# A one-layer hybrid decoder trunk: the S5 read-out in two calls of four column groups instead of four calls of two, and three pieces of work in another order

## The chip, the cores and the metric

The kernel runs on one core of a Trainium2 chip. The metric is the device time of one execution in microseconds (us). Before the change the median of three runs is 482.74 us (482.57 to 483.27). One further execution was profiled; every row below is from it, and it took 482.97 us.

A core has five engines with instruction streams of their own: PE (TensorE, matrix products), DVE (VectorE), ACT (ScalarE), POOL (GpSimd) and SP (SyncE, which only issues DMAs here). They wait for each other through semaphores, which are written out by hand in this kernel. Within an engine the order of the program is the order of execution.

## The reference, cut to what matters

The layer takes x (256 tokens by 1024) and 256 memory tokens. One input projection feeds four groups of 256 channels each: S5 (a diagonal complex state-space model), mLSTM, RWKV-7 and MoBA attention. Each group is normed, they are joined and projected out; then come a cross-attention into the memory and a SwiGLU feed-forward.

The part that the change rewrites is the last step of S5. The complex states are read out through `c`:

```
y = (jnp.einsum('blgp,ghp->blgh', xs_re, c_re) - jnp.einsum('blgp,ghp->blgh', xs_im, c_im))
y = y.reshape(bsz, seq, GW) + d_skip * u
z = jax.nn.gelu(y)
return z * jax.nn.sigmoid(z @ w_glu + b_glu)
```

RWKV-7 is computed in two chunks of 128 tokens with a triangular inverse that is built level by level (levels 1 to 5, then a corner). MoBA has one block of 256 keys here, so it is causal attention with a relative bias.

## The kernel before, in words

**Weights.** Each weight is split into a high part (ACT, `high_part`, L379) and a rest (DVE, `rest`, L385, one instruction of 128x1024), and a product is three passes: high by high, high by rest, rest by high. The splits go through few buffers, so that ACT waits for PE to have used one, DVE for ACT, and PE for DVE. `rests(n)` on DVE and `highs(n)` on ACT do the splits up to the n-th half weight.

**S5 before the read-out.** 1024 complex states are eight tiles of 128. They are handled in four pairs, q = 0 to 3. For each pair PE makes the driving terms (`s5_in`), ACT copies them out, POOL (DVE for q = 2) turns them by the angle of the time (`rotate`), DVE scans them over time (`scan(q)`, L1879 and L1880, four instructions), and POOL turns them back (`rotate_back(q)`, L1166, four products of 128x512 into `pr`). `rotate_back(1)` also waits for `h_rest` 4, which DVE signals behind the second four of its `mem_rest` instructions (L1945, the rest of the normed memory).

**The read-out.** `s5_out(q, b)` on PE takes the two state tiles of pair q and makes their 32 output channels each, in bank 3: four terms for each tile, eight matmuls of 128 rows by 32 columns of weights with 256 moving columns. Each writes 32 of the 128 output partitions (a column group of the array); two groups are in use in one call. A float32 matmul is two records in the profile, so a call is 16 records. It waits for `rotated_back` q + 1. `rotate_back(q)` overwrites `pr` and waits for `s5_out_used` q in its turn, so read-outs and turns alternate.

**RWKV levels.** `level_p(n, c, b)` on PE waits for `rw_level_mask`, which POOL's `level_mask(n)` (L1176, two instructions) signals; `level_x(n, c)` follows and DVE's `level_update(n)` (L1906, L1908) subtracts. On POOL the order is: `rotate_back(0)`, mask 3, `rotate(1)`, mask 4, `rotate_back(1)`, mask 5, `rotate_back(2)`, `rotate(3)`, `rotate_back(3)`.

**PE's order around the change** (L780 to L900): level 2's `level_x`; `s5_out(0)`; level 3's `level_p`; the transposes `g_col` (L804) and the rows `max_row` for mLSTM; the projection `mb_v`; level 3's `level_x`; `wkv(0)` in two halves (the keys of the memory) with level 4 between; `s5_out(1)`; `ml_qk(2)`, `ml_qk(3)`; level 5's `level_p`; `wkv(1)`; ... `mb_scores(0)` to `(2)`; `s5_out(2)`; `mb_scores(3)`; `solve_u(0)`; first half of `wkv(3)`; `S0`; `bonus`; `s5_out(3)`; second half of `wkv(3)`; ... `values_low(0)`; `solve_u(1)`; `values_low(1)`.

**DVE's order around the change** (L2056 to L2100): the RWKV right side (L2022), the last scan `scan(3)`, `corner()` (L1915, two instructions), `mem_keys(2)` (L1954, the copy of the third quarter of the keys), `mb_biased(0)` to `(2)` (L2033, L2034), a weight rest (L385), `mb_biased(3)`, `solution(0)` (L2026, the first RWKV solution's copy out of its bank, which PE's `S0` waits for), and two reductions (L2064, L2065) that give `mb_max`. ACT's eight exponentials wait for `mb_max`; behind them on ACT stands the weight high of `values_low(0)`. DVE goes on with the S5 output's GELU (L2078 to L2088), and the weight rest that `values_low(1)` needs stands behind those.

Of the kernel before, what the change touches and what calls it, by code (L numbers as in the profile page):

```python
# [14 lines left out]
T = 256  # L15
# [71 lines left out]
def trunk_kernel(nc, x_t, x_rows, mem_t, consts_d, params_d, weights_d, gains_d, rel_scratch, out):  # L87
    ctx = ExitStack()
    with ctx:
# [84 lines left out]
        bu, pr = v4(bu_, 2, T), v4(pr_, 2, T)  # L174
# [130 lines left out]
        def free_of(name):  # L305
            return free[uses[name][0]]
# [105 lines left out]
        def _(pe):  # L412
# [145 lines left out]
            def s5_out(q, b):  # L558

                o = pe_open(pe, "s5_y", b) if q == 0 else bank[b]  # L560
                pe.wait_ge(S["rotated_back"], q + 1)
                for n, (w, x) in enumerate(((c_re, 0), (c_nre, 1), (c_im, 2), (c_im, 3))):
                    for i in (2 * q, 2 * q + 1):
                        y = o[32 * (i % 4):32 * (i % 4) + 32, (i // 4) * T:(i // 4 + 1) * T]
                        last = mm(y, w[:, i, :], pr[:, x, i % 2, :], n == 0, n == 3)
                last.then_inc(full[b] if q == 3 else S["s5_out_used"], 1)
# [230 lines left out]
            s5_out(0, 3)  # L797

            level_p(3, 0, 4)
            level_p(3, 1, 6)  # L800
# [16 lines left out]
            for h in range(NH):  # L817
                max_row(h)
            split_values(11, "mb_v", 0, h_split)
# [12 lines left out]
            s5_out(1, 3)  # L832
# [4 lines left out]
            level_p(5, 1, 6)  # L837
            wkv(1, 1)
# [25 lines left out]
            s5_out(2, 3)  # L864

# [15 lines left out]
            s5_out(3, 3)  # L881
# [235 lines left out]
        def _(pool):  # L1117
# [39 lines left out]
            def rotate_back(q):  # L1157

                cq, sq = cos[:, 2 * q:2 * q + 2, :], sin[:, 2 * q:2 * q + 2, :]
                pool.wait_ge(S["scanned"], q + 1)  # L1160
                if q == 1:
                    pool.wait_ge(S["h_rest"], 4)
                if q > 0:
                    pool.wait_ge(S["s5_out_used"], q)
                for x, (a_, b_) in enumerate(((cq, t1), (sq, t2), (cq, t2), (sq, t1))):
                    last = g.tensor_tensor(pr[:, x], a_, b_, ALU.mult)  # L1166
                last.then_inc(S["rotated_back"], 1)
# [33 lines left out]
        def _(act):  # L1201
# [194 lines left out]
            level_evac(3)  # L1396
            o = wait_full(act, "g_col")
            a.activation(gcol, o[:, 0:8], ACT.Copy).then_inc(free_of("g_col"), 1)
            highs(H_WKV + 1)
# [259 lines left out]
        def _(dve):  # L1659
# [393 lines left out]
            scan(3)  # L2053
            corner()
            mem_keys(2)
            mb_biased(0)  # L2056
            mb_biased(1)
            mb_biased(2)
            rests(H_WKV + 8)
            mb_biased(3)  # L2060
            solution(0)
# [372 lines left out]
```

## Time and profile before

| what | us |
|---|---|
| median of three runs | 482.74 |
| the profiled execution | 482.97 |
| its span, first to last instruction | 481.2 |
| PE busy | 471.1 (98%) |
| DVE busy | 345.4 (72%) |
| ACT busy | 270.6 (56%) |
| POOL busy | 108.4 (23%) |

The span is 1.8 us shorter than the time of the same execution. PE's matmuls are pipelined, and the end of each is modelled, so busy PE doesn't say that no wait is hidden. A row of the timeline gives start and length, engine, line, operation, out<-in, how many were merged, and in brackets the idle time of the engine just before it with what ended it. All of PE's products in the stretch are on one line (L414, a helper), so they are told apart by their tiles and shapes: 128*32 is a read-out, 64*64 an RWKV level. The chain of waits follows the work that ended last back through what released it.

### The profile page before, as it was taken

What the parts mean: (1) busy time and instruction counts of PE and PEld (TensorE: products, weight loads), DVE (VectorE), ACT (ScalarE), POOL (GpSimd) and SP (SyncE); (2) the same over time, 40 slices, a digit from 0 to 9 for tenths busy, and PEclk for the clock granted to TensorE, in tenths of its full rate; (3) what the DMA queues carried; (4) which work ended last, traced back from release to release, by engine and by line L of the source; (5) the groups of instructions that cost most, each with busy time, mean ns of one, the idle gap of its engine ahead of it and who ended that gap; (6) DMA issues with size and microseconds to landing.
All of it is one profiled execution on the core that took longest, in us unless ns stands there. A gap on an engine that the chain in (4) does not pass through costs nothing.

```text
span 481.2 us, 8231 instructions
## 1 busy us (share of the span) xinstructions
PE 471.1 (98%) x3330; PEld 409.0 (85%) x3330; DVE 345.4 (72%) x488; ACT 270.6 (56%) x442; POOL 108.4 (23%) x75
## 2 busy tenths in 40 slices
PE   8999999999999999999999999999999999999995
PEld 6999888989888877889998887888888888888884
DVE  3899999999889887888455736767676777642234
ACT  5678884417232347679557556655555555453342
POOL 0005427793576600000000000000000000344450
PEclk9999999999999999999999999999999999999999
DMA  7874429221410226263733532465555455455502
GB/s 267 338 314 168 161 89 340 69 99 50 148 71 20 89 89 262 86 246 123 260 116 133 207 143 88 176 218 185 196 209 198 176 176 185 172 194 217 193 0 87
DMA packets 12697, 78.91 MB, mean 164 GB/s; under 512 B 1487, under 2 KB 2164, under 8 KB 4084
## 3 DMA queue, kind: packets, MB, share of 16 engines
q1 hardware_dynamic: 12660, 78.39, 45.4%
q8 instruction: 26, 0.43, 0.4%
q14 instruction: 11, 0.09, 0.1%
HBM read 77.33 MB, written 1.84 MB: 165 GB/s over the span
## 4 chain that ended last, share of the span: by engine, by line
PE 70%; DVE 19%; issue 3%; ACT 3%; DMA 2%; POOL 1%; SPq 1%; DVEq 0%; ACTq 0%
PE bank L414 69%; DVE we_rest L385 3%; DMA ring<-weights 2%; POOL arena L1166 1%; DVE arena L1742 1%; DVE wm_rest L385 1%; DVE bank L1689 1%; ACT we_high L379 1%; ACT arena L1440 1%; DVE arena L2014 1%; DVE wk_rest L385 1%; DVE h L1945 0%; DVE arena L397 0%; DVE arena L1759 0%; DVE arena L1879 0%
## 5 line engine op out<-in xcount | busy, mean ns | idle before, releaser
L414 PE MATMUL bank<-h,w_high 128*128 128x512 f32 (+1 forms) x392 | 120.4, 372 | 0.0
L379 ACT ACTIVATE w_high<-ring 128x1024 fp32r<-128x1024 f32 x63 | 66.2, 1058 | 62.7 <-PE bank L414 59.2
L385 DVE TENSOR_TENSOR w_rest<-ring,w_high 128x1024 fp32r<-128x1024 f32 x51 | 63.3, 1245 | 49.2 <-ACT w_high L379 49.0
L414 PE MATMUL bank<-h,w_rest 128*128 128x256 f32 x320 | 89.6, 280 | 0.0
L414 PEld LDWEIGHTS bank<-h,w_high 128*128 128x128 f32 x392 | 68.7, 188 | 13.6 <-issue 0.4
L385 POOL TENSOR_TENSOR w_rest<-ring,w_high 128x1024 fp32r<-128x1024 f32 x7 | 16.8, 2400 | 259.5 <-ACT w_high L379 259.5
L414 PEld LDWEIGHTS bank<-h,w_rest 128*128 128x128 f32 x320 | 60.5, 189 | 0.0
L414 PE MATMUL bank<-arena 64*64 64x64 f32 (+8 forms) x794 | 51.3, 253 | 1.6 <-POOL arena L1119 1.1
L385 DVE TENSOR_TENSOR w_rest<-third_slot,w_high 128x1024 fp32r<-128x1024 f32 x27 | 32.7, 1222 | 27.3 <-ACT w_high L379 27.2
L414 PEld LDWEIGHTS bank<-arena 64*64 64x64 f32 (+4 forms) x794 | 42.2, 144 | 11.4 <-issue 3.9
L414 PE MATMUL bank<-h,we_high 128*128 128x256 f32 x256 | 47.2, 287 | 2.1 <-DVE we_rest L385 1.6
L379 ACT ACTIVATE w_high<-third_slot 128x1024 fp32r<-128x1024 f32 x30 | 31.2, 1055 | 21.0 <-PE bank L414 20.8
L414 PEld LDWEIGHTS bank<-h,we_high 128*128 128x128 f32 x256 | 40.0, 192 | 3.4 <-issue 1.6
L414 PE MATMUL bank<-h,we_rest 128*128 128x256 f32 x128 | 36.2, 283 | 0.0
L414 PE MATMUL bank<-w_high,act_rest 128*128 128x512 f32 x80 | 31.1, 389 | 0.0
L414 PE MATMUL bank<-w_rest,act_high 128*128 128x512 f32 x80 | 31.1, 389 | 0.0
L414 PE MATMUL bank<-w_high,act_high 128*128 128x512 f32 x80 | 31.1, 389 | 0.0
L1166 POOL TENSOR_TENSOR arena<-arena 128x512 f32<-128x512 f32 x16 | 25.0, 1594 | 20.6 <-DVE arena L1880 8.4
L414 PE MATMUL bank<-w_high,h 128*128 128x512 f32 x88 | 27.9, 403 | 0.6 <-DVE w_high L385 0.6
L385 DVE TENSOR_TENSOR we_rest<-ring,we_high 128x1024 fp32r<-128x1024 f32 x18 | 23.9, 1343 | 1.7 <-ACT we_high L379 1.6
L414 PEld LDWEIGHTS bank<-h,we_rest 128*128 128x128 f32 x128 | 24.5, 192 | 0.0
L414 PEld LDWEIGHTS bank<-w_high,h 128*128 128x128 f32 x88 | 16.5, 188 | 4.7 <-DVE w_high L385 0.7
(341 smaller groups left out, 1020.2 us busy)
## 6 DMA issues: line engine op xcount, KB each, us to landing
ring<-weights SPq DMA_DIRECT2D x49, 1024.0 KB, 4.8
third_slot<-weights SPq DMA_DIRECT2D x15, 1024.0 KB, 4.8
gain<-gains SPq DMA_DIRECT2D x3, 512.0 KB, 5.6
cst<-consts SPq DMA_DIRECT2D x1, 1216.0 KB, 8.8
par<-params SPq DMA_DIRECT2D x1, 1168.0 KB, 10.4
kx<-x_t SPq DMA_DIRECT2D x2, 512.0 KB, 5.6
ring<-weights SPq DMA_DIRECT2D x2, 512.0 KB, 6.6
vx<-mem_t SPq DMA_DIRECT2D x1, 1024.0 KB, 9.7
```

What stands on the lines that cost most here:

```text
L379: nc.scalar.activation(split_half(i)[0], raw_half(i), ACT.Copy).then_inc(S["w_high"], 1)
L385: e.tensor_tensor(rest_, raw_half(i), high.bitcast(F32), ALU.subtract).then_inc(rest_done(i)[0], 1)
L414: return nc.tensor.matmul(out_, lhsT, rhs, start=start, stop=stop, skip_group_check=True)
L1166: last = g.tensor_tensor(pr[:, x], a_, b_, ALU.mult)
L1440: e = a.activation(Sm[:, h, lo:hi], Sm[:, h, lo:hi], ACT.Exp, bias=nmax[:, 4 * m + h:4 * m + h + 1], accum_out=mb_sum[:, 4 * m + h:4 * m + ...
L1689: v.tensor_tensor(o, o, copies(rstd_x[0:rows_], n), ALU.mult).then_inc(S["x_scaled"], 1)
L1742: last = v.scalar_tensor_tensor(cv[:, i, d:T], o[:, c, 0:T - d], cw[:, i, 3 - d:4 - d], cv[:, i, d:T], ALU.mult, ALU.add)
L2014: v.reciprocal(den, den).then_inc(S["ml_den"], 1)
```

## The change

- **PE:** `s5_out` takes j = 0, 1 in place of q. A call waits for `rotated_back` 2j + 2, covers four state tiles, and each of its four terms goes to four column groups (output partitions 32g, g = 0 to 3). `s5_out(0)` now stands behind level 5's `level_p`, and `s5_out(1)` where `s5_out(3)` was; two of the four places are gone. Level 3's `level_p` moves behind `g_col` and `max_row`.
- **POOL:** `rotate_back` writes to two buffers in turn, `pr` and the space of `vx` (which holds the memory until its split is done). `rotate_back(1)` waits for no read-out any more; `(2)` and `(3)` wait for `s5_out_used` 1.
- **ACT:** the copy of `g_col` comes ahead of the copies of level 3's products.
- **DVE:** `scan(3)` moves behind `corner()` and `mem_keys(2)`; `solution(0)` moves ahead of a weight rest and `mb_biased(3)`.

The number of matmuls, of POOL's products and of DVE's and ACT's instructions stays the same.

```diff
-        bu, pr = v4(bu_, 2, T), v4(pr_, 2, T)
+        bu = v4(bu_, 2, T)
+        prs = [v4(pr_, 2, T), v4(flat(vx), 2, T)]
...
-            def s5_out(q, b):
-
-                o = pe_open(pe, "s5_y", b) if q == 0 else bank[b]
-                pe.wait_ge(S["rotated_back"], q + 1)
+            def s5_out(j, b):
+
+                o = bank[b] if j else pe_open(pe, "s5_y", b)
+                pe.wait_ge(S["rotated_back"], 2 * j + 2)
                 for n, (w, x) in enumerate(((c_re, 0), (c_nre, 1), (c_im, 2), (c_im, 3))):
-                    for i in (2 * q, 2 * q + 1):
-                        y = o[32 * (i % 4):32 * (i % 4) + 32, (i // 4) * T:(i // 4 + 1) * T]
-                        last = mm(y, w[:, i, :], pr[:, x, i % 2, :], n == 0, n == 3)
-                last.then_inc(full[b] if q == 3 else S["s5_out_used"], 1)
+                    for g in range(4):
+                        last = mm(o[32 * g:32 * g + 32, j * T:(j + 1) * T], w[:, 4 * j + g, :],
+                                  prs[g // 2][:, x, g % 2, :], n == 0, n == 3)
+                last.then_inc(full[b] if j else S["s5_out_used"], 1)
...
             level_x(2, 1)
-            s5_out(0, 3)
-
-            level_p(3, 0, 4)
-            level_p(3, 1, 6)
...
             for h in range(NH):
                 max_row(h)
+            level_p(3, 0, 4)
+            level_p(3, 1, 6)
             split_values(11, "mb_v", 0, h_split)
...
             level_x(4, 1)
-            s5_out(1, 3)
...
             level_p(5, 1, 6)
+            s5_out(0, 3)
             wkv(1, 1)
...
             mb_scores(2, 2)
-            s5_out(2, 3)
-
             mb_scores(3, 5)
...
-            s5_out(3, 3)
+            s5_out(1, 3)
             wkv(3, 1, (1,))
...
-                if q > 0:
-                    pool.wait_ge(S["s5_out_used"], q)
+                if q > 1:
+                    pool.wait_ge(S["s5_out_used"], 1)
                 for x, (a_, b_) in enumerate(((cq, t1), (sq, t2), (cq, t2), (sq, t1))):
-                    last = g.tensor_tensor(pr[:, x], a_, b_, ALU.mult)
+                    last = g.tensor_tensor(prs[q % 2][:, x], a_, b_, ALU.mult)
...
-            level_evac(3)
             o = wait_full(act, "g_col")
             a.activation(gcol, o[:, 0:8], ACT.Copy).then_inc(free_of("g_col"), 1)
+            level_evac(3)
...
             solve_rhs(0)
-            scan(3)
             corner()
             mem_keys(2)
+            scan(3)
             mb_biased(0)
             mb_biased(1)
             mb_biased(2)
+            solution(0)
             rests(H_WKV + 8)
             mb_biased(3)
-            solution(0)
```

PE's order at the second read-out, before. The first row is the last of level 4's `level_x`; the rows of 32x256 are `s5_out(1)`, those that wait for `ml_qk` are `ml_qk(2)` and `(3)`, and those that wait for `rw_level_mask` are the two calls of level 5's `level_p`.

```order
L414 MATMUL bank<-arena 64x64 [waits bank_free6]
L414 MATMUL bank<-arena 64x64 x7
L414 MATMUL bank<-arena,par 32x256 [waits rotated_back]
L414 MATMUL bank<-arena,par 32x256
L414 MATMUL bank<-arena 32x256 x2
L414 MATMUL bank<-arena,par 32x256 x4
L414 MATMUL bank<-arena 128x256 [waits ml_qk,bank_free2]
...
L414 MATMUL bank<-arena 64x64 [waits bank_free5,rw_level_mask,bank_free4]
L414 MATMUL bank<-arena 64x64 x7
L414 MATMUL bank<-arena 64x64 [waits bank_free7,rw_level_mask,bank_free6]
L414 MATMUL bank<-arena 64x64 x7
L414 MATMUL bank<-h,wm_high 128x256 [waits w_rest_mid,bank_free1]
```

And PE's order in the same place after the change, from level 5's second `level_p` on:

```order
L415 MATMUL bank<-arena 64x64 [waits bank_free7,rw_level_mask,bank_free6]
L415 MATMUL bank<-arena 64x64 x7
L415 MATMUL bank<-arena,par 32x256 [waits rotated_back,bank_free3]
L415 MATMUL bank<-arena,par 32x256
L415 MATMUL bank<-vx,par 32x256 x2
L415 MATMUL bank<-arena 32x256 x2
L415 MATMUL bank<-vx,arena 32x256 x2
L415 MATMUL bank<-arena,par 32x256 x2
L415 MATMUL bank<-vx,par 32x256 x2
L415 MATMUL bank<-arena,par 32x256 x2
L415 MATMUL bank<-vx,par 32x256 x2
L415 MATMUL bank<-h,wm_high 128x256 [waits w_rest_mid,bank_free1]
```

The read-out of eight matmuls ahead of `ml_qk(2)` is gone, and one of sixteen, half of them from `vx`, stands between level 5's products and `wkv(1)`.

DVE's order before, from the RWKV right side (the row that waits for `bank_full5`) to the reductions. The rows that wait for `rw_top` are `corner()`, the row into `kx` is `mem_keys(2)`, the COPY is `solution(0)`.

```order
L2022 TENSOR_SCALAR arena<-bank 128x256 [waits bank_full5]
L1879 SCALAR_TENSOR_TENSOR arena<-small,arena 128x256 [waits rotating]
...
L1915 TENSOR_SCALAR arena<-bank 64x256 [waits rw_top,bank_full4]
L1915 TENSOR_SCALAR arena<-bank 64x256 [waits rw_top,bank_full6]
L1954 TENSOR_TENSOR kx<-bank,arena 128x512 [waits rstd_m,bank_full1]
...
L385 TENSOR_TENSOR w_high<-ring,w_high 128x1024 [waits w_high]
L2033 SCALAR_TENSOR_TENSOR arena<-bank,small,arena 128x128 [waits rstd_col,rel_in,bank_full5]
L2034 SCALAR_TENSOR_TENSOR arena<-bank,small,arena 128x256
L2026 COPY arena<-bank 128x256 [waits bank_full4]
L2064 TENSOR_REDUCE small<-arena 128x4 [waits bank_free2,bank_free5,bank_free0,bank_free7]
```

And after:

```order
L2019 TENSOR_SCALAR arena<-bank 128x256 [waits bank_full5]
L1912 TENSOR_SCALAR arena<-bank 64x256 [waits rw_top,bank_full4]
L1912 TENSOR_SCALAR arena<-bank 64x256 [waits rw_top,bank_full6]
L1951 TENSOR_TENSOR kx<-bank,arena 128x512 [waits rstd_m,bank_full1]
L1876 SCALAR_TENSOR_TENSOR arena<-small,arena 128x256 [waits rotating]
...
L2023 COPY arena<-bank 128x256 [waits bank_full4]
L386 TENSOR_TENSOR w_high<-ring,w_high 128x1024 [waits w_high]
L2030 SCALAR_TENSOR_TENSOR arena<-bank,small,arena 128x128 [waits rstd_col,rel_in,bank_full5]
L2031 SCALAR_TENSOR_TENSOR arena<-bank,small,arena 128x256
L2061 TENSOR_REDUCE small<-arena 128x4 [waits bank_free2,bank_free5,bank_free0,bank_free7]
```

The scan has gone behind three instructions, and the copy ahead of the weight rest; the work between the right side and the reductions is the same.

## Rows read from the trace of the kernel before

**Rows 1.** The page, parts 1 and 2: busy times, and PE's granted clock in tenths.

```profile
PE 471.1 (98%) x3330; PEld 409.0 (85%) x3330; DVE 345.4 (72%) x488; ACT 270.6 (56%) x442; POOL 108.4 (23%) x75
...
PEclk9999999999999999999999999999999999999999
```

**Rows 2.** The chain of waits: start, us, what.

```profile
119.55 6.00 POOL arena L1166 x4
...
125.60 16.76 PE bank L414 x212
...
310.69 165.28 PE bank L414 x872
```

**Rows 3.** Timeline of PE: start, us, instruction, [idle before <-releaser].

```profile
35.58 0.47 PE L414 MATMUL bank<-h,we_high 128*128 128x256 f32 x2 [0.97 <-DVE we_rest L385]
...
101.81 1.34 PE L414 MATMUL bank<-arena 64*64 64x64 f32 x32 [0.17 <-DVE arena L1908]
...
104.94 0.47 PE L414 MATMUL bank<-wm_high,h 128*128 128x256 f32 x1
...
125.60 0.62 PE L414 MATMUL bank<-arena,par 128*32 128x256 f32 x4 [0.58 <-POOL arena L1166]
...
127.45 2.01 PE L414 MATMUL bank<-arena 64*128 64x256 f32 x40
129.39 0.50 PE L414 MATMUL bank<-h,wm_high 128*128 128x256 f32 x2
...
161.45 0.63 PE L414 MATMUL bank<-arena,par 128*32 128x256 f32 x4
...
171.78 1.28 PE L414 MATMUL bank<-arena 64*64 64x64 f32 x16
173.62 0.50 PE L414 MATMUL bank<-w_high,h 128*128 128x512 f32 x1 [0.56 <-DVE w_high L385]
```

**Rows 4.** Timeline of POOL.

```profile
101.60 5.38 POOL L1152 TENSOR_TENSOR arena<-arena 128x512 f32<-128x512 f32 x1
...
108.31 1.30 POOL L1155 TENSOR_TENSOR arena<-arena 128x512 f32<-128x512 f32 x1
...
126.10 0.64 POOL L1176 TENSOR_TENSOR arena<-arena,cst 128x256 f32<-128x256 f32 x1
...
148.91 1.29 POOL L1155 TENSOR_TENSOR arena<-arena 128x512 f32<-128x512 f32 x1
154.83 5.98 POOL L1166 TENSOR_TENSOR arena<-arena 128x512 f32<-128x512 f32 x4 [4.64 <-PE bank L414]
157.29 2.29 POOL L1166 TENSOR_TENSOR arena<-arena 128x512 f32<-128x512 f32 x1
```

**Rows 5.** Timeline of DVE.

```profile
102.34 1.21 DVE L385 TENSOR_TENSOR wm_rest<-ring,wm_high 128x1024 fp32r<-128x1024 f32 x1
...
109.34 1.34 DVE L385 TENSOR_TENSOR wm_rest<-ring,wm_high 128x1024 fp32r<-128x1024 f32 x1 [0.70 <-ACT wm_high L379]
...
117.76 1.66 DVE L1945 SCALAR_TENSOR_TENSOR h<-vx,par,h 128x256 fp32r<-128x256 f32 x4
...
149.20 2.08 DVE L385 TENSOR_TENSOR wm_rest<-ring,wm_high 128x1024 fp32r<-128x1024 f32 x1
...
153.88 0.72 DVE L1915 TENSOR_SCALAR arena<-bank 64x256 f32<-64x256 f32 x2
...
155.12 0.33 DVE L2033 SCALAR_TENSOR_TENSOR arena<-bank,small,arena 128x128 f32<-128x128 f32 x1
...
157.07 1.35 DVE L385 TENSOR_TENSOR w_high<-ring,w_high 128x1024 fp32r<-128x1024 f32 x1
...
159.00 0.41 DVE L2026 COPY arena<-bank 128x256 f32<-128x256 f32 x1
159.33 0.67 DVE L2064 TENSOR_REDUCE small<-arena 128x4 f32<-128x512 f32 x1
159.92 1.20 DVE L2065 TENSOR_REDUCE small<-arena 128x4 f32<-128x1024 f32 x1
```

## The prediction

> **What bounds the kernel now.** The page first. PE is busy for 471.1 of 481.2 us and its granted clock is full in all 40 slices [rows 1]. That invites the reading that every microsecond taken from PE is one won. The chain of waits tests it. Its last piece is 165.28 us of products from 310.69 on [rows 2]: there PE alone sets the time, and whatever shift it has on entering is carried to the end. In the stretch that the change touches (99 to 174 us), the chain goes through POOL's `rotate_back(1)` at 119.55 to PE at 125.60 [rows 2]. So third, the waits: PE's timeline shows its two real stops there, 0.58 us before the read-out at 125.60 (POOL) and 0.56 us before 173.62 (DVE's weight rest) [rows 3]. At 173.62 PE is late because DVE is. The question is therefore what the change does to the DVE and POOL work that ends there, not what it does to PE's sum.
>
> Fourth, the two timelines side by side, since DVE and POOL hold each other up. DVE's weight rest takes 1.21 us undisturbed (102.34). The one at 109.34 takes 1.34, the one at 149.20 2.08, the one at 157.07 1.35 [rows 5]. POOL's product open at each start ends at 109.61, 150.20 and, as the next one starts at 157.29, about 157.3 [rows 4]. Each rest ends 1.08 us behind that (110.68, 151.28, 158.42). In the other direction POOL's product at 157.29 takes 2.29 and ends 1.16 behind the rest. So whichever is under way finishes, and the other then needs its own time less some 0.15. A DVE rest that comes early into an open POOL product wins nothing.
>
> **The change part by part.** A read-out call takes 1.85 us of PE (125.60 to 127.45 [rows 3]). Four calls become two. If four column groups run side by side as two do, a call still takes 1.85: PE's work falls by 3.70 us. If they run as pairs, one after the other, two calls take what four did: 0. I take 1.85 and keep both ends. By stretch:
>
> 1. *99.7 to 104.9, first read-out gone, level 3 behind the rows.* `mb_v` starts at 104.94 and could start 1.85 and the wait of 0.17 earlier, at 102.92 at best. Its first half frees the buffer whose rest DVE starts at 109.34, behind 0.70 us of idling [rows 5]. DVE could start at 108.64. But POOL's product at 108.31 is open until 109.61 [rows 4], so the rest would end at 110.69, as before. Gain 0; bounds 0 and 0.70. ACT's copy of `g_col` ahead of level 3's copies only keeps `max_row` supplied, and has the same cover.
>
> 2. *To the second read-out.* DVE has no idle time from there to the end of its memory rests at 119.42 (117.76 + 1.66), where `h_rest` 4 releases `rotate_back(1)` on POOL at 119.55 [rows 2, 5]. Both are unchanged. POOL ends it at 125.55 and makes level 5's masks until 126.74 (126.10 + 0.64 [rows 4]). PE no longer waits for the turn, but its new neighbour, level 5's `level_p`, waits for the mask: even with no gain before, PE would be there at 125.02 (125.60 less the stop) plus 0.86 for the `ml_qk` pair. The second half of `level_p` starts at 126.80, takes 0.62 (under half of the 1.34 of such a pair [rows 3]), and the first new read-out 1.85: `wkv(1)` starts at 129.27, where it was 129.39 [rows 3]. Gain 0.1. The stop has changed its releaser, and what was removed ahead of it is spent waiting.
>
> 3. *129 to 151.3.* The 0.1 travels with PE to DVE's mLSTM output. There the rest at 149.20 is held by POOL's product from 148.91 to 150.20 [rows 4, 5], and that one hangs on `scan(2)` and `rotated_back` 2, which have not moved. The rest ends at 151.28 either way. Gain 0. The same 0.9 us of holding would swallow most of a loss of that size.
>
> 4. *151.3 to 161.1, DVE's new order.* `corner` and `mem_keys(2)` take 1.24 (153.88 to 155.12 [rows 5]). With the last scan behind them, `scanned` 4 comes at 155.19, not 153.95. POOL's `rotate_back(3)` used to start at 154.83, kept from starting by the third read-out on PE [rows 4]; now it starts at 155.27, 0.44 later, so removing that wait is more than given back. Its third product would start near 157.73, and its second ends at 157.78. DVE now does `solution(0)` first (0.33, 159.00 to 159.33 [rows 5]), comes to the rest at 157.39, is held to 157.78 and ends it at 158.86, before at 158.42. `mb_biased(3)` follows (0.65) and the reductions can start at 159.55 instead of 159.33; they end at 161.34 instead of 161.12 (159.92 + 1.20). Loss 0.22.
>
> 5. *The last read-out.* POOL's turn takes 5.98 [rows 4] with one rest in it: `rotated_back` 4 at 161.25. PE has by then lost one call and moved up by about 2 us, so it waits some 1.8 us in front of `s5_out(1)` and starts it at 161.3, before at 161.45 [rows 3]. The copy of the first solution ends at 157.47 and PE needs it at about 157.8: no stop. Gain 0.15 on PE, which reaches the old stop at 172.9 (before 171.78 + 1.28 = 173.06 [rows 3]).
>
> 6. *161.3 to 173.6.* ACT's exponentials, DVE's reciprocal, the S5 output and two rests follow `mb_max` without a change, and POOL's work among them hangs on the same signal. The rest comes 0.22 later, PE resumes at 173.84, and the stop grows from 0.56 to about 0.95.
>
> Sum: 0.22 later on the path: 482.97 + 0.22 = 483.2 for such a profiled execution. That one stood 0.23 above the median, so 482.9 to 483.0 for a median of runs. No DMA is moved past another; SP's order is the same.
>
> One rule of the Trainium skill bears on terms 1 and 3. In SBUF — State Buffer, "SBUF: two separate sides", a DVE instruction with two SBUF inputs and a GpSimd instruction that reads SBUF exclude each other for the whole instruction, whoever starts first. By that rule the gain of term 1 is 0. One pair of rows speaks against it: the rest at 102.34 takes 1.21 although POOL's L1152 is open from 101.60 to 106.98 [rows 4, 5], where three other pairs agree. If term 1 went by that pair, its gain would be 0.70; this is the second rival.
>
> **The rivals.**
>
> *A, nothing won (forecast).* Terms as above: 482.9, own range 482.4 to 483.5.
>
> *B, POOL doesn't hold DVE at 108.6.* The rest starts 0.70 earlier, the memory rests and POOL's turn and masks with it, and the whole rhythm moves up; less term 4's 0.22 it is 0.5: 482.2. For it: the pair at 102.34. Against: the three others, and that POOL's delayed product would then hold the memory rests behind it.
>
> *C, PE's work counts.* If the masks don't bind (POOL ahead of what its rough spans show), PE comes to `wkv(1)` earlier by the first call with its wait (2.0), the second with its stop (2.4), less one new call (1.85): 2.6. DVE's 0.2 off: 480.4. For it: PE at 98%. Against: `h_rest` 4 at 119.42, which POOL cannot pass, and DVE without a gap before it.
>
> *D, slower: the four groups run as two pairs.* Each call is 3.6. The first sends PE on 1.6 later, of which DVE's output keeps about 0.5 after the holding at 149.2; the last starts at 161.7 instead of 161.3 and ends at 165.3. PE then comes to the stop near 174.9, later than the rest, so PE decides: 1.3 later, 484.1. It decides as soon as a call costs over about 2.8 us. For it: no row shows four tiles of 128 rows at once. Against: two such tiles take the time of one now. In TensorE: Matmul & The Clock Gate, "Measured speedup vs the span model", three column tiles run 2.38 times as fast as in turn; by that the call would be some 2.3, and the sum the same.
>
> *E, slower: the clock falls in the new idle time of 1.8 us.* The longest stop now is 0.97 (35.58 [rows 3]) with the clock at full level. At the lower level (1.2 GHz for 2.4) PE's 11 us to the stop would take twice that: some 494.
>
> **How the numbers follow.** A 0.57, B 0.14, C 0.12, D 0.13, E 0.02, and 0.02 for what isn't listed. This kernel can tell about 0.2% (0.97 us) from no change: faster is below 481.8, slower above 483.7. Faster takes C and a little of B: 0.15. Slower takes D, E and the tail of A: 0.20. No change: 0.65. The range reaches down past B and halfway to C, and up over D: 481.4 to 484.3, which leaves out most of C, E and odd cases, under 0.2 in all.
>
> **What would show it.** In the changed profile: each read-out call 1.85 to 1.9 us long with four starts a few nanoseconds apart (against D); the rest of `wkv(0)`'s first half starting near 108.6 and ending at 110.7 (against B); PE's stop before level 5's `level_p`, released by POOL's L1173, with the mask ending near 126.7 (against C); `wkv(1)` at 129.3; DVE's rest at about 157.4 ending near 158.9; `mb_max` at 161.3; PE idle for 1.8 us before the last read-out, at full clock; PE's stop at 173.8 nearly 1 us long. I am wrong if `rotate_back(1)` starts before 119.4, or if `mb_max` comes before 161.

## The result, and the profile after

| | median us | lowest to highest | runs |
|---|---|---|---|
| before | 483.04 | 482.51 to 483.52 | 20 |
| changed | 483.56 | 482.94 to 484.46 | 20 |

The ratio is 1.0014, 95% interval 1.0008 to 1.0021: 0.4 to 1.0 us slower. I had forecast 0.2 slower (482.9, range 481.4 to 484.3, no measurable change the likeliest). The direction held, the range held, and the size was too small. The profiled execution of the changed kernel took 483.12, with a span of 481.3, 0.1 over that of before. Yet it ran 0.23 us ahead when it came to the changed stretch: the weight rest near 42 us, where both kernels are the same, starts at 41.75 instead of 41.98 already. So I measure from a mark that both have: the start of the weight rest near 102 us (102.34 before, 102.11 after).

The page's busy times and granted clock, which answer to [rows 1]:

```profile
PE 468.0 (97%) x3330; PEld 407.3 (85%) x3330; DVE 345.9 (72%) x488; ACT 270.5 (56%) x442; POOL 108.4 (23%) x75
...
PEclk9999999999999999999999999999999999999998
```

PE is busy for 3.1 us less. The four column groups do run side by side. PE's timeline at the two read-outs and at the two stops, which answers to [rows 3]:

```profile
126.03 1.28 PE L415 MATMUL bank<-arena 64*64 64x64 f32 x32 [0.73 <-issue]
127.24 0.41 PE L415 MATMUL bank<-arena,par 128*32 128x256 f32 x2
127.26 0.41 PE L415 MATMUL bank<-vx,par 128*32 128x256 f32 x2
127.48 0.39 PE L415 MATMUL bank<-arena,par 128*32 128x256 f32 x2
...
129.11 0.50 PE L415 MATMUL bank<-h,wm_high 128*128 128x256 f32 x2
...
157.39 0.70 PE L415 MATMUL bank<-arena 128*64 128x64 f32 x16 [0.45 <-DVE arena L2023]
158.02 1.13 PE L415 MATMUL bank<-arena,cst 128*128 128x512 f32 x2
161.12 0.41 PE L415 MATMUL bank<-arena,par 128*32 128x256 f32 x2 [1.97 <-POOL vx L1163]
...
173.82 0.73 PE L415 MATMUL bank<-w_high,h 128*128 128x512 f32 x2 [1.07 <-DVE w_high L386]
```

A call runs from 127.24 to 129.11, 1.87 us, and the pair from `arena` and the pair from `vx` start together. That rules out rival D. What PE gained comes back as idle time, which stands in brackets: 0.73 ahead of level 5's products, 0.45 ahead of `S0`, 1.97 ahead of the last read-out, 1.07 ahead of `values_low(1)` (before 0.56). Two more stops of 0.44 and 0.65 us, at 103.47 and 112.96, are new as well; both are released by DVE. The profile puts down no engine as the releaser of the 0.73 ("issue"), where I had said POOL's mask. The rows still fit the mask: its two instructions end at 125.93 and 126.53, and the two halves of level 5's products start 0.10 behind each.

The chain of waits, which answers to [rows 2] (start, us, what):

```profile
117.61 1.59 DVE h L1942 x4
...
119.34 5.97 PE bank L415 x96
125.31 0.73 issue
126.03 16.05 PE bank L415 x220
...
148.99 1.66 DVE wm_rest L386
...
157.21 1.50 DVE w_high L386
...
160.10 1.22 DVE small L2062
...
161.35 1.03 ACT arena L1437 x5
```

The chain no longer passes through POOL's turn at 119.55. From 142 to 161.3 no engine but DVE is on it. POOL's and DVE's timelines at the places of [rows 4, 5]:

```profile
148.71 1.30 POOL L1152 TENSOR_TENSOR arena<-arena 128x512 f32<-128x512 f32 x1
155.10 5.96 POOL L1163 TENSOR_TENSOR vx<-arena 128x512 f32<-128x512 f32 x4 [5.09 <-DVE arena L1877]
156.35 1.28 POOL L1163 TENSOR_TENSOR vx<-arena 128x512 f32<-128x512 f32 x1
157.59 2.25 POOL L1163 TENSOR_TENSOR vx<-arena 128x512 f32<-128x512 f32 x1
```

```profile
108.33 2.14 DVE L386 TENSOR_TENSOR wm_rest<-ring,wm_high 128x1024 fp32r<-128x1024 f32 x1
...
148.99 2.10 DVE L386 TENSOR_TENSOR wm_rest<-ring,wm_high 128x1024 fp32r<-128x1024 f32 x1
...
156.88 0.40 DVE L2023 COPY arena<-bank 128x256 f32<-128x256 f32 x1
157.21 1.50 DVE L386 TENSOR_TENSOR w_high<-ring,w_high 128x1024 fp32r<-128x1024 f32 x1
158.64 0.34 DVE L2030 SCALAR_TENSOR_TENSOR arena<-bank,small,arena 128x128 f32<-128x128 f32 x1
158.90 0.47 DVE L2031 SCALAR_TENSOR_TENSOR arena<-bank,small,arena 128x256 f32<-128x256 f32 x1
159.50 0.69 DVE L2061 TENSOR_REDUCE small<-arena 128x4 f32<-128x512 f32 x1
160.10 1.21 DVE L2062 TENSOR_REDUCE small<-arena 128x4 f32<-128x1024 f32 x1
```

The rest at 108.33 starts 6.21 behind the mark, where it was 7.00, and takes 2.14: it ends at 110.47, 8.35 behind the mark; before it was 8.34. The rest at 157.21 is held until 157.63 and ends at 158.71.

**Three marks for all runs.** Between four points the traces repeat to 0.02 us, so that single executions can be compared: the start of the rest near 102; the start of the rest near 149; the end of the second reduction; the first product of `values_low(1)`. The pieces between them are a, b and c. Behind the last of the points the traces are alike again: 307.5 to 307.6 us to the end of the span in thirteen of the fourteen. Ahead of the first they are not: it comes between 101.9 and 103.4 us, and that scatter is in every median. The last columns are the median and ratio over all runs (before, on the same chips, 482.94 to 483.07).

| kernel | a | b | c | median | ratio, 95% interval |
|---|---|---|---|---|---|
| before | 46.86 | 11.92 | 12.50 | | |
| changed | 46.88 | 12.32 | 12.51 | 483.56 | 1.0014, 1.0008 to 1.0021 |
| DVE's old order | 46.89 | 11.79 | 12.50 | 482.92 | 0.9997, 0.9988 to 1.0006 |
| before with DVE's new order | 46.87 | 12.29 | 12.51 | 483.33 | 1.0009, 1.0001 to 1.0018 |
| scan put back | 46.89 | 12.30 | 12.50 | 483.25 | 1.0009, 1.0000 to 1.0018 |
| solution put back | 46.89 | 11.80 | 12.50 | 483.50 | 1.0009, 1.0000 to 1.0018 |
| solution put back, again | 46.89 | 11.79 | 12.51 | 483.42 | 1.0008, 0.9999 to 1.0017 |
| masks first | 46.42 | 12.44 | 12.50 | 483.39 | 1.0010, 1.0001 to 1.0018 |
| first read-out twice | 48.32 | 12.06 | 12.51 | 484.51 | 1.0039, 1.0026 to 1.0052 |
| last read-out later | 46.89 | 12.32 | 12.50 | 483.13 | 1.0014, 1.0004 to 1.0025 |
| solution one place earlier | 46.89 | 12.31 | 12.76 | 483.81 | 1.0020, 1.0011 to 1.0029 |
| changed, again | 46.89 | 12.32 | 12.51 | 483.69 | 1.0014, 1.0005 to 1.0023 |
| rest behind the reductions | 46.88 | 10.89 | 12.50 | 481.83 | 0.9977, 0.9969 to 0.9986 |
| the same, masks first | 46.42 | 11.01 | 12.50 | 481.96 | 0.9977, 0.9967 to 0.9986 |

The changed kernel loses 0.02 in a, 0.40 in b and nothing in c. That is 0.4 of the measured 0.5 (by the medians) to 0.7 (by the ratio); the remainder is not in its profile. The section on the granted clock below has the likeliest source for it.

### The profile page after: what moved, and what is told of

Read it like the earlier page. It is cut to its first block, busy times and chain, and to the rows that moved or that the text cites. A ratio compares the mean times of both kernels' runs of the same rounds, so it can differ in the third digit from the quotient of the medians.

```text
span 481.3 us, 8231 instructions
## 1 busy us (share of the span) xinstructions
PE 468.0 (97%) x3330; PEld 407.3 (85%) x3330; DVE 345.9 (72%) x488; ACT 270.5 (56%) x442; POOL 108.4 (23%) x75
## 4 chain that ended last, share of the span: by engine, by line
PE 67%; DVE 8%; issue 1%; ACT 1%; DVEq 0%
PE bank L415 66%; DVE wm_rest L386 1%; DVE h L1942 1%; ACT arena L1437 1%; DVE arena L2011 1%; DVE w_high L386 1%; DVE arena L1877 1%; DVE wk_rest L386 0%; PE bank L943 0%; PE bank L974 0%; DVE arena L1876 0%; DVE arena L2081 0%; DVE arena L1964 0%; DVE arena L2031 0%; PE bank L653 0%
## 5 line engine op out<-in xcount | busy, mean ns | idle before, releaser
L415 PE MATMUL bank<-arena 64*64 64x64 f32 (+6 forms) x786 | 50.1, 253 | 2.7 <-POOL arena L1116 1.1
L415 PEld LDWEIGHTS bank<-arena 64*64 64x64 f32 (+3 forms) x786 | 41.8, 145 | 11.4 <-issue 4.2
L2137 DVE TENSOR_TENSOR xtmp<-bank,gain 128x512 f32<-128x512 f32 x12 | 8.3, 691 | 16.5 <-ACT px L1488 16.4
```

The source lines that it names most:

```text
L415: return nc.tensor.matmul(out_, lhsT, rhs, start=start, stop=stop, skip_group_check=True)
L2137: v.tensor_tensor(xtmp[:, m, cs], o[:, :], gain_[:, cs], ALU.mult).then_inc(free_of(f"{tag}{i}"), 1)
```

## The experiments

### Which part of the change costs b its 0.40

**DVE's old order in the changed kernel.** Both pieces of DVE go back to where they were.

```diff
             solve_rhs(0)
+            scan(3)
             corner()
             mem_keys(2)
-            scan(3)
...
-            solution(0)
             rests(H_WKV + 8)
             mb_biased(3)
+            solution(0)
```

> The changed kernel with DVE's order of before: scan(3) ahead of corner() and mem_keys(2), solution(0) behind mb_biased(3). Theory L (DVE and POOL hold each other, whichever is under way finishes first): the scan ends 1.24 us earlier, rotate_back(3) starts near 153.9 with no read-out to wait for, its third product is open when the weight rest comes at about 156.9 and until about 157.6, so the rest ends near 158.7 as in the changed kernel; solution(0) then adds 0.33 behind it, and the reductions end near 161.6. Expected about 483.7, 0.2 to 0.3 above the changed kernel's 483.5, 0.6 above before. Rival O (the order of DVE costs what was forecast and nothing else does): the loss goes with the order: 483.0, no difference to before, reductions ending at 161.1. Rival R (the read-out's new form and place cost it): 483.6 whatever DVE's order is, but with the reductions at 161.1 and the loss elsewhere.

Measured: no difference to before, b 11.79. The loss is gone, as rival O said, and my theory L was wrong about why: the rest was not held.

```profile
157.14 1.21 DVE L386 TENSOR_TENSOR w_high<-ring,w_high 128x1024 fp32r<-128x1024 f32 x1
...
158.53 0.47 DVE L2031 SCALAR_TENSOR_TENSOR arena<-bank,small,arena 128x256 f32<-128x256 f32 x1
158.92 0.41 DVE L2023 COPY arena<-bank 128x256 f32<-128x256 f32 x1
159.25 0.67 DVE L2061 TENSOR_REDUCE small<-arena 128x4 f32<-128x512 f32 x1
```

```profile
156.56 2.92 POOL L1163 TENSOR_TENSOR vx<-arena 128x512 f32<-128x512 f32 x1
```

POOL's product had been open for 0.58 us, and the rest still took its undisturbed 1.21; the product ended 1.14 behind the rest's end. There is a second difference to the rows of after: the reduction starts at 159.25, while the COPY still runs, and not 0.13 behind `mb_biased(3)`.

**DVE's new order in the kernel before.**

```diff
             solve_rhs(0)
-            scan(3)
             corner()
             mem_keys(2)
+            scan(3)
...
+            solution(0)
             rests(H_WKV + 8)
             mb_biased(3)
-            solution(0)
```

> The kernel before with DVE's new order alone (corner() and mem_keys(2) ahead of scan(3), solution(0) ahead of the weight rest and mb_biased(3)); read-outs as before. Theory L: scanned 4 comes at 155.2 (before 153.95), after the third read-out, so rotate_back(3) starts at 155.27, its second product holds the rest to 157.78, and the reductions end 0.2 to 0.4 later than before: 483.2 to 483.4, ratio 1.0004 to 1.0010. Rival O says the same 0.2 to 0.4. Rival R: no loss, 483.0, ratio 1.0000.

Measured: b 12.29, so DVE's order alone costs 0.37 and the read-out's new form 0.03 on top. With DVE's old order the new form is even 0.13 ahead (11.79 against 11.92), because there the rest near 157 isn't held. Rival R is out.

**One piece at a time.** The scan put back:

```diff
             solve_rhs(0)
+            scan(3)
             corner()
             mem_keys(2)
-            scan(3)
```

> The changed kernel with scan(3) ahead of corner() and mem_keys(2) again, solution(0) still early. Theory L: rotate_back(3) starts near 153.9, the rest comes at 157.2 while its third product is open until 157.6, and ends near 158.7 as in the changed kernel: 483.5, within 0.1 of the changed kernel; what the scan's place does is only to choose which product holds the rest. Rotated_back 4 comes 1.2 earlier, so that PE's idle time ahead of the last read-out falls from 2.0 to about 0.8 us, at no gain in time. Rival O (the scan's place is the loss): 483.1. Rival I (PE's idle time of 2 us is what costs): the loss halves, 483.2.

The solution put back, in two runs of the same kernel:

```diff
-            solution(0)
             rests(H_WKV + 8)
             mb_biased(3)
+            solution(0)
```

> The changed kernel with solution(0) behind mb_biased(3) again, scan(3) still late. Theory L: the rest comes 0.33 earlier, at 156.88, is held by the same product of rotate_back(3) until 157.6, and ends at 158.7 as in the changed kernel; solution(0) then stands on the path to the reductions, 0.33 more: 483.8 to 483.9. PE's S0 comes later (it waits for that copy, at about 159.8), still ahead of the last read-out at 161.1. Rival O: the same rest ends 0.33 earlier, so nothing changes: 483.5. Rival R: 483.5.

> The kernel with the solution put back, once more. Its first profiled execution was its fastest, 482.48, with the rest ahead of POOL's product; its median was 483.50. Theory V (who goes first differs from execution to execution): another profile can show the rest held, 1.5 us and more, and 12.6 from the rest near 149 to the reductions' end. Theory K (that stretch is the same in every execution, and executions differ by when their first products start): 11.80 again within 0.02, whatever its time; median 482.9 to 483.1 and the first one's 483.5 a matter of its executions' starts.

Measured: with the scan put back b stays at 12.30, as theory L said (PE loses its time elsewhere than L had it: it stops for 1.52 ahead of `solve_u(0)`, which now waits for the later `corner()`, and not at all ahead of the last read-out); with the solution put back it falls to 11.80 and 11.79, where L had said 12.65. So the whole 0.4 hangs on where the solution's copy stands (its place is worth 0.52 in b), and the scan's place is worth nothing. It hangs on it in two ways, both in the rows. The second run of the solution put back, DVE and then POOL:

```profile
156.88 1.21 DVE L386 TENSOR_TENSOR w_high<-ring,w_high 128x1024 fp32r<-128x1024 f32 x1
...
158.67 0.40 DVE L2023 COPY arena<-bank 128x256 f32<-128x256 f32 x1
159.00 0.67 DVE L2061 TENSOR_REDUCE small<-arena 128x4 f32<-128x512 f32 x1
```

```profile
156.35 2.86 POOL L1163 TENSOR_TENSOR vx<-arena 128x512 f32<-128x512 f32 x1
```

First, without the copy the rest comes 0.53 us after the start of POOL's product and takes 1.21; with the copy it comes 0.33 later, 0.86 after that start, and takes 1.50. Second, the copy behind `mb_biased(3)` filled the time in which the reduction waits for that instruction's result, so that it adds only 0.10 there. Together that is 0.33 + 0.29 - 0.10 = 0.52.

Theory K held against V: the second run shows the same b. Who goes first is fixed by the order of work. The medians (483.50, 483.42) lie 0.5 above what b says; see the clock below.

**Is it the neighbour or the distance?**

```diff
             mb_biased(1)
+            solution(0)
             mb_biased(2)
-            solution(0)
             rests(H_WKV + 8)
```

> The changed kernel with solution(0) one place earlier, between mb_biased(1) and mb_biased(2), so that the weight rest follows directly on mb_biased(2), as in the kernel with the solution put back, but starts as late as in the changed kernel. In the traces so far the rest waited for POOL's open product when the COPY stood right ahead of it and it started 0.86 to 0.90 us behind the product's start, and went first where mb_biased(2) stood right ahead of it and it started 0.53 to 0.58 behind. Theory W (what stands right ahead of the rest decides): the rest goes first, 1.2 us, and the reductions end 0.3 us earlier than in the changed kernel: from the rest near 149 to the reductions' end 12.0 instead of 12.32, 483.1 to 483.2. Theory T (how far the product has come decides): it is held, 1.5 us, 12.32, 483.5.

```profile
157.24 0.47 DVE L2031 SCALAR_TENSOR_TENSOR arena<-bank,small,arena 128x256 f32<-128x256 f32 x1
157.63 1.50 DVE L386 TENSOR_TENSOR w_high<-ring,w_high 128x1024 fp32r<-128x1024 f32 x1
```

```profile
156.77 1.28 POOL L1163 TENSOR_TENSOR vx<-arena 128x512 f32<-128x512 f32 x1
```

Measured: with `mb_biased(2)` right ahead of it the rest is still held, 1.50 us, b 12.31. Theory W is out. The rows fit T: in the fourteen traces, this weight rest is held where it starts 0.85 us or more behind the product's start, and not held at 0.53 to 0.58. The distance was not varied by itself, and the last section shows that it is not the rule elsewhere.

### Is what PE gains or loses ahead of 149 us kept?

**Level 5's masks ahead of `rotate_back(1)`,** so that PE's stop of 0.73 goes.

```diff
             level_mask(4)
+            level_mask(5)
             rotate_back(1)
-            level_mask(5)
```

> The changed kernel with level 5's masks ahead of rotate_back(1) on POOL, so that PE's level_p(5) has nothing to wait for (the stop of 0.73 us at 126.03, released by POOL's L1173). Theory A (as forecast for the terms ahead of 151 us: what PE gains there is kept by POOL's product at 149): the stop goes, the rest at 149 comes 0.7 earlier, but ends where it did: no difference to the changed kernel, 483.4 to 483.5; the time from the weight rest near 102 to that near 149, 46.87 in the traces so far, falls to 46.2, and the time from there to the reductions' end grows by as much. Rival G (the rest now comes into the product before the last one, is held by that alone and gets in ahead of the last one): it ends 1.3 earlier, 482.3. Rival N (nothing gained at 126 arrives at 149 either): 46.87 stays, 483.5.

Measured: a is 0.46 shorter and b 0.12 longer, 0.34 won in the trace, between A and G. The stop of 0.73 is gone, which shows that it was the mask's. The median and the ratio (1.0010 for 1.0014) don't tell this kernel from the changed one. Two things that I had not seen: the masks now run beside DVE's memory rests and delay `h_rest` 4, so that PE waits 1.04 us ahead of 120.48 (it was 0.28); and the rest at 148.89 came into the last but one product (L1151, from 148.73), waited for it and went ahead of the last:

```profile
148.89 2.21 DVE L386 TENSOR_TENSOR wm_rest<-ring,wm_high 128x1024 fp32r<-128x1024 f32 x1
```

**The first read-out made twice.**

```diff
                 pe.wait_ge(S["rotated_back"], 2 * j + 2)
-                for n, (w, x) in enumerate(((c_re, 0), (c_nre, 1), (c_im, 2), (c_im, 3))):
+                terms = ((c_re, 0), (c_nre, 1), (c_im, 2), (c_im, 3))
+                for n, (w, x) in [(n, t) for _ in range(2 - j) for n, t in enumerate(terms)]:
                     for g in range(4):
```

> The changed kernel with the matmuls of s5_out(0) made twice (same result), 1.86 us more of PE at 127.2. Theory A: the rest at 149 comes 1.86 later, at 150.85, when POOL's last product is done at 150.0, so it takes 1.2 instead of 2.1 and ends 0.95 later: 484.4 to 484.5. Rival P (PE's work there is on the path in full): 485.3. Rival F (PE's work is not on the path at all there): 483.5. It also prices the call: 1.86 us with four column groups side by side, 3.7 if they went as pairs.

```profile
150.46 1.22 DVE L386 TENSOR_TENSOR wm_rest<-ring,wm_high 128x1024 fp32r<-128x1024 f32 x1
```

Measured: counted from the mark, PE comes to `wkv(1)` 1.74 later and the rest 1.44 later (a); no longer held, it takes 1.22, and b falls by 0.26. The sum is 1.2 by the marks and by the ratios (1.0039 for 1.0014), and 0.95 by the medians, where A had said 0.95 and P 1.86. The medians rest on five runs here. So a loss there is kept but for what the waits behind it absorb.

**The last read-out behind the second half of `wkv(3)`,** so that PE has work while it waits.

```diff
-            s5_out(1, 3)
             wkv(3, 1, (1,))
+            s5_out(1, 3)
```

> The changed kernel with s5_out(1) behind the second half of wkv(3), so that PE has work in the 1.97 us in which it waited for rotated_back 4. Theory A (DVE sets the end of the stretch): PE is through sooner and only waits longer at 173.8, 3 us instead of 1.07: 483.5, no difference to the changed kernel. Rival C (PE's idle time ahead of the read-out costs): up to 1.07 less, 482.5. Rival E (the clock: in the execution profiled of the kernel with the scan put back, the granted clock was 0.50 from 174 to 178 us behind stops of 0.24, 0.28 and 1.19 us, at 485.02): a stop of 3 us makes that more frequent, median 485, with the granted clock under 0.7 behind 173.8.

Measured: a, b and c as in the changed kernel. Filling PE's idle 1.97 us wins nothing in these pieces; it comes back as stops of 1.32, 0.30 and 1.19. The median is 483.13, 0.43 under that of the changed kernel, while the ratio is the same 1.0014. The marks give no reason for a gain; a chance in the starts of these twelve runs, or a low clock in fewer of them (next section), could be one, and the runs don't decide it.

### The granted clock

In two of the fourteen profiles the granted clock fell to 0.50, the lower of the two levels, within the work. (It is at 0.50 in the last 0.1 to 3.3 us of the span as well, in all fourteen; that alone makes mean clocks of 0.997 to 1.000.) The last columns of such a row are the granted clock, the DMA share and GB/s. The solution one place earlier, where PE is idle for 2.46 us, from 159.07 to 161.53:

```profile
160.00:162.00 2.00, 0.47 (x8) 0.75 0.89 254
162.00:164.00 2.00, 2.00 (x24) 0.50 0.69 283
164.00:166.00 2.00, 2.00 (x22) 0.89 0.00 0
```

The scan put back, behind stops of 0.24, 0.28 and 1.19 us, with the stop's row first:

```profile
174.08 0.50 PE L415 MATMUL bank<-w_high,h 128*128 128x512 f32 x1 [1.19 <-DVE w_high L386]
```

```profile
174.00:176.00 2.00, 1.92 (x6) 0.69 0.33 94
176.00:178.00 2.00, 2.00 (x7) 0.50 0.95 397
178.00:180.00 2.00, 2.00 (x26) 0.96 0.13 41
```

From the rows, the time at half clock is 3.4 us in both: (0.25 x 2 + 0.50 x 2 + 0.11 x 2) x 2 in the first. Half of that, 1.7 us, is what it costs a PE that is at work all the time. In the first, 0.5 of the 3.4 us lay in PE's idle time (half clock from about 161.0), so that some 1.45 was lost; PE's later stop, 1.07 in the changed kernel, took up most of it, and c grew by 0.25. In the second the clock fell some 0.7 us after PE was back at work, and no stop lay behind it: the stretch behind the last mark took 309.13 where it takes 307.5 to 307.6 in the others, 1.56 more, and the execution took 485.02.

**The changed kernel once more** is the last run of this part.

> The changed kernel itself once more, on the chip of the other three. Theory K: 46.87 from the rest near 102 to that near 149, 12.32 from there to the reductions' end, 12.50 to the first product of values_low(1), within 0.02 each, whatever the execution's time; median 483.3 to 483.6, ratio to before 1.0007 to 1.0014. Theory V: one of the three differs by over 0.3. Rival E (the granted clock falls behind the stops of 2 and 1.07 us in part of the executions): a few executions 1.5 us over the rest.

Its profile repeats a, b and c, with the same stops (1.97 and 1.08) and a full clock. But every run also gives its mean granted clock. In the two profiles with the fall it is 0.995 and 0.996; in the twelve without it is 0.997 to 1.000. So I take 0.996 or less as the sign of a fall within the work; that this holds in the executions that were not profiled is inferred. Sorted by that:

| kernel | stops of PE over 0.5 us behind 149 | runs at 0.996 or less | their median, and that of the others |
|---|---|---|---|
| before | 0.56 | 0 of 93 | 482.94 to 483.07 |
| before with DVE's new order | 0.94 | 0 of 11 | 483.33 |
| changed, both series | 1.97, 1.07 | 15 of 31 | 484.0, 483.4 |
| solution put back, both | 2.24, 0.79 | 14 of 22 | 483.6, 482.7 to 483.0 |
| solution one place earlier | 2.46 | 8 of 11 | 484.0, 483.6 |
| masks first | 1.98, 1.08 | 6 of 11 | 483.6, 483.2 |
| scan put back | 1.52, 1.19 | 6 of 11 | 483.5, 483.1 |
| first read-out twice | 1.90, 1.08 | 1 of 5 | 485.8, 484.5 |
| DVE's old order | 1.52, 0.69, 0.82 | 2 of 11 | 482.8, 482.9 |
| last read-out later | 1.32, 1.19 | 2 of 12 | 485.3, 483.1 |
| rest behind the reductions (both) | 1.0, 0.63 | 0 of 20 | 481.8, 482.0 |

So the changed kernel's 483.56 is two groups: executions at full clock, 483.4, which is 0.35 above before and what a and b say, and nearly half at 484.0, whose mean clock says that it fell for a while. If it fell at the 1.97 us stop, PE's later stop of 1.07 took up most of the 1.7 us. Both the fall and its place are inferred here; no profile of the changed kernel itself caught one. That PE's stops bring it is an argument from the table (0 of 93 before, 0 of 31 in the three other kernels whose stops stay at about 1 us or less, some in every kernel with a stop of 1.3 us or more), not from a run that changed nothing else. Why the same stops bring it in one execution and not in the next was not tried here. The Trainium skill (TensorE: Matmul & The Clock Gate, "Part 1: The HAM clock gate (the "warmup" mystery)") says of the cold products at a kernel's start that the chip's watch on PE's activity runs free of that start, so that their number differs from run to run of one kernel. That 15 of 31 executions show a fall and 16 don't would fit such a watch, but no run here tests it.

### A version that beats both

DVE's rest moves behind the reductions, into the time in which DVE waited for ACT.

```diff
             solution(0)
-            rests(H_WKV + 8)
             mb_biased(3)
...
             v.tensor_reduce(nmax[:, 4:8], Sm[:, :, P:P + T], AX.X, ALU.max, negate=True).then_inc(S["mb_max"], 1)
+            rests(H_WKV + 8)
```

> The changed kernel with DVE's weight rest rests(H_WKV + 8) behind the two reductions instead of ahead of mb_biased(3). Theory A (DVE's work up to mb_max sets the time of the stop at 173.8): the rest's 1.5 us (1.2 and the holding) go from the path, the reductions end at 159.8 instead of 161.3, DVE makes the rest in the time in which it waited for ACT's exponentials, and everything up to the stop at 173.8 comes 1.1 to 1.3 earlier, until PE's own work binds; PE needs the rest at about 163.3, it ends at 161. 482.2 to 482.4, ratio to before 0.9982 to 0.9989. Rival Q (the stop at 173.8 is set by another chain, ACT's weight highs or a weight's transfer): under 0.3 of gain, 483.2 to 483.5.

DVE's timeline, POOL's turn, and PE's last stop:

```profile
158.80 0.69 DVE L2060 TENSOR_REDUCE small<-arena 128x4 f32<-128x512 f32 x1
159.41 1.21 DVE L2061 TENSOR_REDUCE small<-arena 128x4 f32<-128x1024 f32 x1
160.53 1.36 DVE L386 TENSOR_TENSOR w_high<-ring,w_high 128x1024 fp32r<-128x1024 f32 x1
```

```profile
155.83 4.98 POOL L1163 TENSOR_TENSOR vx<-arena 128x512 f32<-128x512 f32 x4 [5.09 <-DVE arena L1877]
```

```profile
173.12 0.73 PE L415 MATMUL bank<-w_high,h 128*128 128x512 f32 x2 [0.63 <-DVE w_high L386]
```

Measured: b is 1.43 shorter than in the changed kernel, c unchanged, ratio to before 0.9977. POOL's turn is not disturbed either (4.98 us for four products instead of 5.96), PE's stop ahead of the read-out is 0.99, and no run shows the low clock. Theory A held, and more was won than it said (481.83 for 482.2 to 482.4): b alone gained 1.43 where it had said 1.1 to 1.3, and the part of the changed kernel's median that goes with the low clock went as well.

With the masks first on top:

> The kernel with the weight rest behind the reductions, with level 5's masks ahead of rotate_back(1) as well. The two gains lie in different pieces of the chain (10.89 instead of 12.32 from the rest near 149 to the reductions' end; 0.34 less from the rest near 102 to there), so they should add: 0.3 less than the rest behind the reductions alone, 481.5, ratio to before 0.9970. Rival S (PE's own work binds once 1.8 us are gone: its stop at 173.1 was still 0.63): no rival down to that; 481.5 as well. Rival H (the earlier rest at 149 holds POOL's last product and so the last scan): the gain is lost, 481.8.

Measured: a and b together are 0.34 shorter again in its trace, but the medians (481.96 with 9 runs, 481.83 with 11) and ratios don't tell the two apart.

## Why the prediction was right, and where it was not

**Term 1, the first read-out gone: right.** The rest started 0.79 nearer the mark (forecast 0.70) and was held to the same end. Rival B is refuted by the 2.14 us at 108.33.

**Term 2, the stop that changes its releaser: right.** Forecast: the masks end at 126.74, `wkv(1)` at 129.27. Measured, with the 0.23 by which this execution ran ahead: 126.76 and 129.34. Rival C is refuted: the stop is there, and it went when the masks were moved. That `rotate_back(1)` starts at 119.33, under my limit of 119.4, is the same shift (17.22 behind the mark, before 17.21).

**Term 3, nothing gained at 149: right.** Piece a is the same in both kernels to 0.02. The reason I gave for it, that the holding swallows gains, held only in part: with the masks first 0.34 of 0.46 came through in the trace.

**Term 4, DVE's new order: right in sign, 0.22 forecast, 0.38 measured** (from the end of the rest at 149 to the reductions' end, 9.85 before, 10.23 after). I had put the reductions 0.69 behind the rest's end; they start 0.79 behind it, because the moved copy no longer stands between `mb_biased(3)` and the instruction that waits for it. The rest's end was 0.04 off, the reductions 0.02. The reasoning also named the wrong piece: it gave the loss to the scan, which starts POOL's turn 0.44 later, and the scan's place costs nothing. What makes the rest late is the copy ahead of it, which also brings it to POOL's product at a distance at which it has to wait. The rule behind this term, that whichever is under way finishes first, failed in three traces (the rest at 0.53 to 0.58). By the same rule I expected the solution put back to be 0.3 slower still, and its b fell by 0.52. That the changed kernel is one where the rule holds, and that the sign came out, is in part luck.

**Terms 5 and 6: right.** PE idle for 1.97 instead of 1.8, its last stop 1.07 instead of 0.95, c unchanged; `values_low(1)` 0.2 later than forecast, the error of term 4.

**Rival D, a call as two pairs: refuted** by four starts within 20 ns and by 1.87 us a call, which is also well under the 2.3 that the prediction gives beside it.

**Rival E, the clock: this is the step that failed.** I gave it 0.02 and a time of some 494, from "PE's 11 us to the stop would take twice that". By the mean clock it happened in about half of the executions (15 of 31). It lasted 3.4 us both times that a profile shows it, which is 1.7 of PE at most, and the executions with it are 0.6 us slower in the median, since PE had a stop ahead. My only evidence was that a stop of 0.97 had left the clock at full level [rows 3]; I had no row for twice that and should have given it more chance and a bound from below. From the forecast 482.9 to the median 483.56: 0.3 is that the kernel before has 483.04 over 20 runs where three had given 482.74, 0.16 is term 4, and the remaining 0.1 to 0.2 is what the low clock puts on the median (483.56 with it, 483.4 without).

## What to carry to other kernels

Where PE waits for another engine, work taken from PE can return as idle time and win nothing, as 3.1 us did here; and the kernels with stops of 1.3 to 2.5 us were the ones that showed the lower clock in part of their executions. Look for what stands on the waiting chain without being needed there: one weight rest moved behind the two reductions took 1.4 us from it, where 3.1 us less of PE took none. Before moving a small instruction, ask what it covers: the copy was free between a result and its reader, and elsewhere it cost 0.4.

## What the runs showed of the hardware

By the starts that the traces record, DVE and POOL, which hold each other up, are not simply served in the order in which they came. Where a weight rest starts while one of POOL's products is open, it ends 1.08 us behind that product's end in 94 pairs of the fourteen traces, wherever in the product it came (0.01 to 1.11 us behind its start). But in the three traces in which it came 0.53 to 0.58 behind the start of `rotate_back(3)`'s product, and in all fourteen at 102, 0.74 to 0.76 behind the start of L1149 (L1152 before), it went first. In the three the product ended 1.12 to 1.14 behind the rest; at 102 a second rest and one more DVE instruction passed as well, and the product took 5.38 us instead of 1.3. Between them lie pairs at 0.61 to 0.63 (the rest at 121) that were held. So the distance goes with the outcome among kernels that are alike at that place, and no threshold follows from it; what does decide was not found. POOL's spans are rough in the profile, so the start that it records need not be the moment at which the product began to exclude the rest. The Trainium skill (SBUF — State Buffer, "SBUF: two separate sides") has it that whichever of the two starts first gets the shared ports for the whole instruction. Most pairs agree with that; by the recorded starts these seventeen don't, and here the measurement decides.

Four column groups with 128 rows of state each run side by side: four starts within 20 ns, the next four 0.22 to 0.24 us later, and the call takes 1.87 us where one of two groups took 1.85.
